# One hybrid decoder layer on Trainium2: the first expert's rows gathered already turned, tile by tile, and the compressed scores of both heads in one product

## The reference, cut to what matters

```python
kc = rms_norm(compress_blocks(kv(k_c), ...), k_norm_g[0])       # 15 compressed keys for each key head
s_c = jnp.einsum('bskgd,bnkd->bkgsn', qg, kc) * scale           # the compressed scores
...
x = x + concat(nsa_out, gla_out) @ w_out
h2 = rms_norm(x, norm2_g)
logits = h2 @ w_router + b_router
top_vals, top_idx = lax.top_k(logits, 4)                        # 4 of 32 experts
...                                                             # rows sorted by expert
hgu = xb @ w_gate_up[e] + b_gate_up[e]                          # 1024 -> 2048
y = clamped_swiglu(hgu) @ w_down[e] + b_down[e]                 # 1024 -> 1024, weighted by the gate and added
```

## Time and profile before

| what | value |
|---|---|
| median of three runs | 1067.37 us |
| the runs | 1065.93, 1067.37, 1068.52 us |
| span of the profiled execution, first to last instruction | 1064.8 us |
| TensorE busy | 1018.3 us, 96% |
| VectorE, ScalarE busy | 293.2 and 167.9 us |
| moved by the transfers | 426.45 MB, 400 GB/s over the span |
| mean granted TensorE clock | 0.996 |

### The profile page before, as it was taken

The page is one execution under the profiler, slowest core; times in us unless marked ns, Lnnn a source line. Parts: engine busy times, 40 slices in busy tenths (PEclk is TensorE's granted clock), DMA queues, the critical chain, the costliest instruction groups (busy, mean ns, idle before and its releaser), DMA issues.

```text
span 1064.8 us, 12012 instructions
## 1 busy us (share of the span) xinstructions
PE 1018.3 (96%) x4969; PEld 410.9 (39%) x4969; DVE 293.2 (28%) x676; ACT 167.9 (16%) x325; POOL 15.9 (1%) x42
## 2 busy tenths in 40 slices
PE   8999999999999999999999999999999999899998
PEld 5555644333333333333333333333333333333334
DVE  1764614222222222211222122222112222222222
ACT  2434321111111111110110011111101111110011
POOL 4100000000000000000000000000000000000000
PEclk9999998999999999999999999999999999999999
DMA  9992668999999999999999999999999999999996
GB/s 295 363 409 84 251 263 320 426 424 435 431 430 430 432 429 431 431 433 432 432 431 430 432 432 433 433 432 429 429 429 429 431 433 431 431 432 431 420 425 264
DMA packets 36023, 426.45 MB, mean 400 GB/s; under 512 B 3782, under 2 KB 12062, under 8 KB 19728
## 3 DMA queue, kind: packets, MB, share of 16 engines
q1 hardware_dynamic: 34224, 424.78, 94.9%
q0 software_dynamic: 704, 1.04, 0.5%
q10 hardware_dynamic: 1056, 0.07, 0.1%
HBM read 424.83 MB, written 1.05 MB: 400 GB/s over the span
## 4 chain that ended last, share of the span: by engine, by line
PE 62%; DMA 34%; DVE 2%; SPq 1%; issue 1%; ACT 0%; ACTq 0%; DVEq 0%
DMA pair<-in_w_down 30%; PE bank L1694 24%; PE bank L1706 14%; PE bank L1316 5%; DMA pair<-in_w_gate_up 4%; PE bank L1728 4%; PE bank L1591 3%; PE bank L1678 2%; PE bank L1720 2%; PE bank L1686 1%; PE bank L1713 1%; PE bank L1388 1%; PE bank L1946 1%; SPq L363 1%; PE bank L1348 1%; DMA stage<-in_w_in 1%
## 5 line engine op out<-in xcount | busy, mean ns | idle before, releaser
L1694 PE MATMUL bank<-pair,xs 128*64 128x512 f32 x2048 | 450.0, 594 | 21.9 <-DMA pair<-in_w_gate_up 20.8
L1694 PEld LDWEIGHTS bank<-pair,xs 128*64 128x64 f32 x2048 | 143.1, 137 | 323.3 <-issue 285.9
L1706 PE MATMUL bank<-pair,sig 128*64 128x512 f32 x960 | 212.2, 593 | 13.4 <-DMA pair<-in_w_down 13.4
L1209 DVE COPY gu<-bank 128x512 f32<-128x512 f32 x32 | 36.5, 1140 | 416.2 <-PE bank L1694 416.2
L1706 PEld LDWEIGHTS bank<-pair,sig 128*64 128x64 f32 x960 | 72.3, 137 | 149.2 <-issue 143.4
L757 ACT COPY gu<-bank 128x512 f32<-128x512 f32 x32 | 36.4, 1138 | 457.1 <-PE bank L1694 457.1
L854 DVE TENSOR_TENSOR xs<-bank,gt 128x512 f32<-128x512 f32 x31 | 21.4, 691 | 220.6 <-PE bank L1686 220.6
L1316 PE MATMUL bank<-stage,xt 128*128 128x512 f32 x160 | 72.2, 598 | 0.0
L1728 PE MATMUL bank<-ys,pgt 64*128 64x512 f32 x248 | 61.6, 615 | 0.3 <-ACT ys L762 0.3
L1678 PE MATMUL bank<-xr,onehot 128*64 128x512 f32 x248 | 58.5, 592 | 0.0
L762 ACT COPY ys<-bank 128x512 f32<-128x512 f32 x31 | 18.1, 585 | 206.2 <-PE bank L1706 206.2
(11 more groups left out here) (310 smaller groups left out, 497.0 us busy)
## 6 DMA issues: line engine op xcount, KB each, us to landing
pair<-in_w_gate_up SPq DMA_DIRECT2D x51, 4096.0 KB, 39.8
pair<-in_w_down SPq DMA_DIRECT2D x24, 4096.0 KB, 38.0
pair<-in_w_gate_up SPq DMA_DIRECT2D x22, 2048.0 KB, 14.6
pair<-in_w_down SPq DMA_DIRECT2D x15, 1024.0 KB, 13.3
pair<-in_w_down SPq DMA_DIRECT2D x6, 2048.0 KB, 32.9
stage<-in_w_in SPq DMA_DIRECT2D x5, 2048.0 KB, 19.2
pair<-in_w_gate_up SPq DMA_DIRECT2D x8, 1024.0 KB, 4.8
stage<-in_w_out SPq DMA_DIRECT2D x2, 2048.0 KB, 15.2
```

Source lines behind the costliest of these rows:

```text
L1209: V.tensor_copy(gu[:, 1, :].rearrange("p (i q) -> p q i", i=FQ), up_banks[1][:].rearrange("p (q i) -> p q i", i=FQ)).then_inc(s["gu_lo"], 1)
L1694: last = mm(up_banks[a][b * CAP:(b + 1) * CAP, :].rearrange("p (q i) -> p q i", i=FQ), xs[:, k, :], cols[:, b], start=k == 0, stop=k == DK ...
L1706: last = mm(down_bank[b * CAP:(b + 1) * CAP, :], actf[:, kk % FQ, kk // FQ, :], row[:, 512 * b:512 * (b + 1)], start=kk == 0, stop=kk == D ...
```

## The change

It has two parts.

**Compressed scores.** `kct` becomes 30 columns wide: columns 0 to 14 hold head 0's keys on partitions 0 to 63, columns 15 to 29 head 1's on 64 to 127, and the rest is zero (a new memset on VectorE). Eight products over all 128 rows take the place of the sixteen; the bank is chosen by the token tile.

**The handover.** The product with the one-hot has its operands exchanged: a 128 x 128 piece of `xr` (by `features`) is stationary and the one-hot of 64 columns moves, so that the gathered rows come out turned, features on the partitions. The ScalarE copies and `first_turn` fall away, and with them the semaphore `xg_first` and two counts of `xfill`. The work goes by token tile: tile 0's position product stands between the two halves of tile 1's router, VectorE makes tile 0's one-hot (`first_hot(0)`) before `choose(1)`, and half of tile 0's gather is issued ahead of the wait for tile 1's mask, the other half after tile 1's position product. The rest of `posm` is made after both one-hots, `first_rows_in` comes ahead of the further rounds of `posm`, the last counting product stands after the first `up_row`, and the memsets of `gates4` and `posm` go ahead of the first residual.

```diff
-        kct = sb("kct", [P, NCMP])
+        kct = sb("kct", [P, HKV * NCMP])
...
+        pos_banks, cnt_bank = (banks[6], banks[1]), banks[2]
...
-            nc.scalar.copy(kct[0:DH, :], banks[5][0:DH, 384:384 + NCMP])
-            nc.scalar.copy(kct[DH:P, :], banks[5][0:DH, 384 + HKO:384 + NCW]).then_inc(s["kct"], 1)
+            nc.scalar.copy(kct[0:DH, 0:NCMP], banks[5][0:DH, 384:384 + NCMP])
+            nc.scalar.copy(kct[DH:P, NCMP:HKV * NCMP], banks[5][0:DH, 384 + HKO:384 + NCW]).then_inc(s["kct"], 1)
...
-            for half, b in enumerate((x_bank, banks[6])):
-                act.wait_ge(s["xfill"], half + 1)
-                nc.scalar.copy(xg[:, 256 * half:256 * (half + 1)], b[:, 0:256]).then_inc(s["xg_first"], 1)
...
-                for half, b in enumerate((x_bank, banks[6])):
+                for half, b in enumerate((x_bank, banks[0])):
...
+            V.memset(kct[:], 0.0)
             V.memset(hidt[:], 0.0).then_inc(s["hid"], 1)
...
+            def first_hot(ti):
+                dve.wait_ge(s["pos_full"], ti + 1)
+                link(V.scalar_tensor_tensor(out=posm[:, ti, 0:1], in0=pos_banks[ti][:, 0:1], scalar=1.0,
+                                            in1=msk[:, ti, 0:1], op0=ALU.add, op1=ALU.mult))
+                V.tensor_scalar(onehot[:, ti, :], iota_f[:], posm[:, ti, 0:1], rs_y[:, ti:ti + 1],
+                                ALU.is_equal, ALU.mult).then_inc(s["onehot" if ti else "oh_first"], 1)
+
+            V.memset(gates4[:, :, ROUNDS * E:], 0.0)
+            link(V.memset(posm[:], 0.0))
             link(V.memset(lg[:, :, E:], FILLER))
             residual(0)
...
             choose(0)
             root(1)
+            first_hot(0)
             choose(1)
...
-            V.memset(gates4[:, :, ROUNDS * E:], 0.0)
-            link(V.memset(posm[:], 0.0))
...
+            first_hot(1)
             for ti in range(NT):
+                for lo, hi, to in ((1, FIRST, 1), (FIRST, E, FIRST + NPAD)):
+                    last = V.scalar_tensor_tensor(out=posm[:, ti, to:to + hi - lo], in0=pos_banks[ti][:, lo:hi],
+                                                  scalar=1.0, in1=msk[:, ti, lo:hi], op0=ALU.add, op1=ALU.mult)
+            link(last)
+            first_rows_in()
...
             for ti in range(NT):
                 for g in range(G):
-                    for h in range(HKV):
-                        last = mm(banks[h][:, ti * 64 + g * NCMP:ti * 64 + (g + 1) * NCMP],
-                                  qt[h * DH:(h + 1) * DH, g, ti * P:(ti + 1) * P], kct[h * DH:(h + 1) * DH, :],
-                                  start=True, stop=True)
+                    last = mm(banks[ti][:, g * HKV * NCMP:(g + 1) * HKV * NCMP], qt[:, g, ti * P:(ti + 1) * P], kct[:],
+                              start=True, stop=True)
...
             route(1, 0, 4)
+            pe.wait_ge(s["msk"], 1)
+            mm(pos_banks[0][:, 0:E], stri[:], msk[:, 0, :], start=True, stop=True).then_inc(s["pos_full"], 1)
             route(1, 4, DK)
+            mm(pos_banks[1][:, 0:E], ones[:], msk[:, 0, :], start=True, stop=False)
+            mm(cnt_bank[:, 0:E], ones[:], msk[:, 0, :], start=True, stop=False)
+
+            def first_gather(ti, half):
+                b = (x_bank, banks[0])[half]
+                for j in range(UP_PIECES):
+                    for i in range(2):
+                        last = mm(b[:, CAP * (2 * j + i):CAP * (2 * j + i + 1)], features(ti, UP_K * j + 2 * half + i),
+                                  onehot[:, ti, :], start=ti == 0 and j == 0 and i == 0, stop=ti == NT - 1,
+                                  skip_group_check=True)
+                return last
+
+            pe.wait_ge(s["oh_first"], 1)
+            first_gather(0, 0)
             pe.wait_ge(s["msk"], 2)
-            mm(banks[6][:, 0:NT * E], stri[:], msk.rearrange("p t e -> p (t e)"), start=True, stop=False)
-            mm(banks[6][:, E:2 * E], ones[:], msk[:, 0, :], start=False, stop=True).then_inc(s["pos_full"], 1)
-            for ti in range(NT):
-                last = mm(banks[4][:, 0:E], ones[:], msk[:, ti, :], start=ti == 0, stop=ti == 1)
-            last.then_inc(s["cnt_full"], 1)
+            mm(pos_banks[1][:, 0:E], stri[:], msk[:, 1, :], start=False, stop=True).then_inc(s["pos_full"], 1)
+            first_gather(0, 1)
+            pe.wait_ge(s["onehot"], 1)
+            first_gather(1, 0).then_inc(s["xt_first"], 1)
+            first_gather(1, 1).then_inc(s["xt_first"], 1)
...
-            first_gather(0, 0)
-            first_gather(0, 1).then_inc(s["xfill"], 1)
-            first_gather(1, 0)
-            first_turn(0)
-            first_gather(1, 1).then_inc(s["xfill"], 1)
             pe.wait_ge(s["xs_first"], 1)
             pe.wait_ge(s["stage4"], 16 * (front_loads(4) + 1))
             up_row(0, 0, up_rows(0)).then_inc(s["rows_used"], 1)
-            first_turn(1)
+            mm(cnt_bank[:, 0:E], ones[:], msk[:, 1, :], start=False, stop=True).then_inc(s["cnt_full"], 1)
             up_row(0, 1, up_rows(0)).then_inc(s["rows_used"], 1)
```

More of the change, by code:

```diff
@@ L266, in decoder_layer @@
             "stage0 stage1 stage2 stage3 stage4 stage5 stage6 down0 down1 wo_low "
-            "ring0 ring1 ring2 ring3 ring4 part0 part1 part2 part3 rows_used used0 used1 used2 used3 used4 xfill oh_first xg_first xt_first xrows xturn xs_first xs oh gu_hi gu_lo up_t glu_in lin_in clamp lin_mul sigm "
+            "ring0 ring1 ring2 ring3 ring4 part0 part1 part2 part3 rows_used used0 used1 used2 used3 used4 xfill oh_first xt_first xrows xturn xs_first xs oh gu_hi gu_lo up_t glu_in lin_in clamp lin_mul sigm "
             "actf onehot pgr pgw slots pgt ys comb tail1 tail2 ").split()}
@@ L764, in rows_out @@
             def rows_out(n):
-                act.wait_ge(s["xfill"], n + 2)
+                act.wait_ge(s["xfill"], n)
                 nc.scalar.copy(xg[:], x_bank[:]).then_inc(s["xrows"], 1)
@@ L863, in first_rows_in @@
                     V.tensor_tensor(xs[:].rearrange("p (b c) n -> p b c n", b=2)[:, :, c, :],
-                                    b[:, 0:256].rearrange("p (c b n) -> p b c n", c=2, b=2),
+                                    b[:, 0:4 * CAP].rearrange("p (b c n) -> p b c n", c=2, b=2),
                                     bc(gt2[:, DK:2 * DK].rearrange("p (b c) -> p b c", b=2)[:, :, c], CAP), ALU.mult)\
@@ L1063, in _ @@
                 for ti in range(NT):
-                    last = V.tensor_tensor(v[:, ti], banks[h][:, ti * 64:ti * 64 + G * NCMP]
-                                           .rearrange("p (g n) -> p g n", g=G),
+                    last = V.tensor_tensor(v[:, ti], banks[ti][:, 0:G * HKV * NCMP]
+                                           .rearrange("p (g h n) -> p h g n", g=G, h=HKV)[:, h],
                                            mcneg[:, ti, :].unsqueeze(1).to_broadcast([P, G, NCMP]), ALU.add)
@@ L1163, in _ @@
             V.tensor_tensor(lgr, lg[:, :, 0:E], bc(ntop, E), ALU.add).then_inc(s["ntop"], 1)
-            V.memset(gates4[:, :, ROUNDS * E:], 0.0)
-            link(V.memset(posm[:], 0.0))
[L1167 to L1171, removed]
-            for ti in range(NT):
-                last = V.tensor_scalar(onehot[:, ti, :], iota_f[:], posm[:, ti, 0:1], rs_y[:, ti:ti + 1],
-                                       ALU.is_equal, ALU.mult)
-                last.then_inc(s["onehot" if ti else "oh_first"], 1)
+            first_hot(1)
+            for ti in range(NT):
+                for lo, hi, to in ((1, FIRST, 1), (FIRST, E, FIRST + NPAD)):
[3 more added lines that the diff above has]
+            first_rows_in()
             for r in range(1, ROUNDS):
@@ L1180, in _ @@
             dve.wait_ge(s["cnt_full"], 1)
-            link(V.reduce_max(rounds_f[:, 0:1], banks[4][:, 0:E], AX.X))
+            link(V.reduce_max(rounds_f[:, 0:1], cnt_bank[:, 0:E], AX.X))
             for r in range(1, ROUNDS):
@@ L1186, in _ @@
             V.tensor_scalar(rounds_i[:, 0:1], rounds_f[:, 0:1], float(GROUPS[0]), None, ALU.add)
-            first_rows_in()
             one_hot(1, 1)
@@ L1237, in step @@
                 lin_out(piece(n, 1), g, it)
-                dve.wait_ge(s["xfill"], it + 3)
+                dve.wait_ge(s["xfill"], it + 1)
                 one_hot(it + 2, at_next)
@@ L1251, in _ @@
             lin_out(piece(0, 1))
-            dve.wait_ge(s["xfill"], 3)
+            dve.wait_ge(s["xfill"], 1)
             one_hot(2, 2)
```

## The result

The changed kernel takes 1070.63 us (median of 5, 1070.3 to 1073.12), the kernel before in the same comparison 1067.18 (1065.93 to 1068.52). It is the second rival that came, the one in which the clock stays down, and the time is 1.5 us beyond the range. The profiled execution took 1070.61, its span is 1068.9, so 1.7 us lie around a span.

A forecast was written before the change was run, and what follows sets the result against it. Expert-weight transfers bound the kernel, their steady start waiting on expert 0's first up_row. Handover 1.4 us plus scores 0.1 gave 1.5 us off: span 1063.3, median 1065.9, rounded up to 1066.0; range 1063.9 to 1069.1.

The forecast's parts named there:

- the second rival: Handover: the clock stays at half until the up rows have run, 1.8 us later less 0.1, 1069.1 us; chance 0.22.
- What bounds the kernel: Before the expert loop: each microsecond the first up_row of expert 0 ends earlier is one at the end, up to 3.4.
- The scores: Compressed scores: eight products take 1.8 us where sixteen took 1.89, gaining 0.1 us (bounds 0 and 0.2).
- The router and the masks: Handover start: router ends about 162.3, tile 1's logits read at 162.50, mask 0.3 us later, tile 0's gathers from 162.6.
- the paragraph on the gathers: Handover: sixteen turned products at 0.22 us each at full clock or 0.43 at half, 3.6 or 6.9 us in all.
- the middle walk: Handover: half clock from 162.7, back at about 166.7, gathers to 168.35, up_row ending 170.1; 1.4 us gained.
- the sum: Whole kernel: 1.4 us from the handover and 0.1 from the scores, giving 1063.3 for the span, 1065.9 for the median.
- no effect: Gathers: products cost 0.43 at either clock, or the clock returns only at 169.5; row ends 171.6, 1067.3 us; chance 0.14.
- The walk for this case: Handover at half clock until the up rows run: gathers end at 169.9, up_row takes 3.4 us, to 173.3; 1.8 us late.
- No fall: Handover: the 1.3 us wait is largely filled, the clock stays full, 3.2 and 0.1 us gained, 1064.1 us; chance 0.22.

The follow-up runs named there:

- neighbouring columns: The changed kernel with each stationary piece of the turned gathers taken from 128 neighbouring columns of xr, not every fourth: 1068.78 us, ratio to before 1.0013.
- the wide products: Eight never-read 512-column products added around the turned gathers of the changed kernel: 1075.47 us; with neighbouring stationary columns 1073.12 us.
- The three distances above: The changed kernel plus eight never-read 512-column products, stationary columns 4, 8 or 16 bytes apart: 1073.12, 1072.69 and 1075.47 us.
- handover only: The kernel before with the new handover alone, scores as before: 1070.26 us, ratio to before 1.0036.
- three versions of the kernel before: The kernel before with one never-read wide product, 1065.78 us; with new scores and that product, 1066.00; with a second, 256-column product too, 1065.86.
- the kernel by tile: The changed kernel's order by token tile and new scores, but the gather unturned as before, with ScalarE copies and transposes: 1067.03 us, ratio 1.0000.
- one wide product: The kernel before plus one never-read 512-column product in TensorE's wait between router and position products: 1065.78 us, ratio 0.9985.

## Why the prediction was wrong, by its own steps

**What bounds the kernel** was right. The end moved with the first issue after the first up row: 2.7 us at that issue, 3.3 at the second expert, 4.1 at the end of the profiled execution. That every microsecond of the first row's end counts once was slightly too simple, because the row after it is also released late while the clock is low (0.64 us).

**The scores** were right in direction: 0.19 us of chain instead of 0.1, inside the bounds. The idle gap that came with them took it back, which the sum did not have; in time nothing that can be measured.

**The router and the masks** were right to 0.2 us: the router's end 162.31 (162.3 forecast), logits read at 162.54 (162.50), tile 0's gathers from 162.76 (162.6).

**The step that failed** is in the paragraph on the gathers: "0.22 and 0.43 are taken, and bounded by these two", for the full and the half clock. It was argued from the router's products, which have the same size, and the paragraph itself says that no row is of exactly this shape. What was not compared was the layout: x1t is read in neighbouring columns, `features` in steps of 16 bytes. Measured, the product costs 0.47 at either clock, above both values. The sixteen take 7.7 us where the middle walk has 5.3 (eight at 0.43, eight mostly at 0.22). The gathers end at 170.63 instead of 168.35, 2.3 us late.

A second term failed with it: the middle walk has the clock back at 166.7 and the first up row at 1.7 us. The clock came back at 175.8 and the row took 3.61, another 1.9 us. Together the row ends at 174.25 instead of 170.1. With the 0.64 us of the second row this is 4.8 us, and the median is 4.7 above the 1065.9 of the sum.

Since the gathers keep their pace at both clocks, the two can be told apart. An estimate for a clock of 1.00 throughout: gathers to 170.63 as measured, an up row of 1.7, an end at 172.3, 0.8 us later than before. So of the 2.7 us at the issue 0.8 are the price of the load and 1.9 the low clock in the up row, and no state of the clock could have made this handover a gain.

The trace of before has a row with this layout, and it would have misled: the transposes of line 1616, whose stationary pieces come from the same `features`. It is the first of these three; the others are the gathers' loads with neighbouring columns, at the full clock with the wide products (337 ns is the very first, at the low clock) and at the half clock without them:

```profile
L1616 PEld LDWEIGHTS bank<-ident,xr x16: 195/208/218, 149.2 to 159.9; 128*128 128x128 f32 x16
L1677 PEld LDWEIGHTS bank<-onehot,xr x32: 190/192/337, 166.4 to 175.8; 128*128 128x128 f32 x32
L1677 PEld LDWEIGHTS bank<-onehot,xr x32: 333/333/333, 162.9 to 169.9; 128*128 128x128 f32 x32
```

The transposes are 0.12 us apart, and those of line 1358, with neighbouring columns, 0.11: the steps of 16 bytes add 0.01 us to a transpose's load and 0.12 to that of a product. Why a transpose is spared no run here shows, so the doubling is shown for the loads of float32 products alone.

The Trainium skill has a rule on this (Advanced Engine Details and Errata, Memory Cachelines, SBUF Cachelines): SBUF is read in lines of 16 bytes, and an access pattern needs at least two hits on a line for the full speed. The three distances above agree with it: two elements to a line 0.88 us, one to a line 1.69. The transposes, with one element to a line and 0.12 us, do not, so the rule alone is not the whole of the cause. The prediction weighed another rule instead, that a load's time is its columns divided by 1.2 and does not shorten with the clock (TensorE: Matmul & The Clock Gate, LDWEIGHTS, in the Trainium skill). For neighbouring columns the trace contradicts the second half: the loads start 0.112 us apart at the full clock and 0.213 at the half clock, and last 192 and 333 ns. For the 16-byte steps the pace is the same at both clocks, 0.233 us. The rival "no effect" named this very case, products of 0.43 at either clock, at a chance of 0.04; its first condition came nearly true (0.47), for another reason than the one it gave, but its time of 1067.3 did not, since it had the up row at the full clock.

**The clock** was the rival that came ("the clock stays down"), and what it says the clock does is seen: the low stretch was 10.2 us and the gathers, without a single gap, did not end it; the clock rose 5.2 us after the up rows of 512 columns had begun. The profiles of handover only and of neighbouring columns show the same order of events: down during or ahead of the gathers, up only under the up rows (175.6 and 172.7). The fall itself came at 165.6, 2.9 us later than the 162.7 of the walk. The walk for this case had the row's end at 173.3 and it came at 174.25. The gathers are 0.8 us dearer (7.67 us for the sixteen, where the half-clock price of 0.43 makes 6.9), they start 0.15 later and the row takes 0.2 more, against 0.25 less for the position product. That the rival's time was this near is luck in part: it had the clock low through all the gathers and none of the load's price. "No fall" was refuted in its premise: the fall came although the 1.3 us wait was filled, so idle time is not needed for it. That the thin work is the cause is supported by the wide products, with which the clock stayed up in some executions, and not proven. The Trainium skill's description of thin kernels that fall back (TensorE: Matmul & The Clock Gate, HAM oscillation) fits in its result; its kernel falls back in waits for transfers, and here there was no wait at all.

**The chances** gave the case that came 0.22, and slower by over 0.2% only 0.16: the price of that case, 1069.1, lay within the 2.1 us, and the range ended at it. With the 0.95 us by which the row ended later than in its walk and the 0.64 of the second row it would have been 1070.7.

## What to carry to other kernels

When operands of a product are exchanged, compare the layout of the new stationary operand and not only its size: in the float32 products here, columns 16 bytes apart doubled the load at the full clock and columns 8 bytes apart added 5%. Products of few moving columns were doubly dear here, for the clock fell to 1.2 GHz under them and the wide work behind them paid for that. Where TensorE must wait after thin work, a wide product whose result nobody reads can be worth trying. In three versions of the kernel before it lowered the median by 1.0 to 1.3 us; only one of the three intervals lies wholly below 1.

## What the runs showed of the hardware that was not expected

- A product with a 128 x 128 float32 stationary operand and 64 moving columns costs, by the starts of its loads, 0.22 to 0.24 us at 2.4 GHz with the stationary columns 4 or 8 bytes apart, and 0.47 with 16. At 1.2 GHz it is 0.43 for neighbours and 0.47 for 16 bytes. The 16 bytes cost 0.04 us at the low clock and 0.24 at the high one. A transpose's load pays 0.01 us for them.
- The clock can fall and stay down under a TensorE without gaps: it is busy at 1.00 in every window from 160 to 176 of the changed kernel, and the granted clock goes to 0.50 in the middle. The executions of the kernel by tile scatter by 4 us with it: 1064.75 at a mean clock of 1.000, 1068.63 at 0.992.
- The 23 executions of the kernel before in the comparison with one wide product have mean clocks of 0.994 to 0.998. With that product, four of eleven have 0.999 or 1.000 and the others 0.996 to 0.998. The highest of the clocks is not always the shortest time.
